# Values' products one step back in TensorE's order, in two attention stages of a three-block model kernel

## The chip, the cores and the metric

The kernel runs on one core of one Trainium2 chip. The metric is the device time of one launch in microseconds. A core has five engines that run their own instruction streams and wait for one another on semaphores: TensorE (PE in the profile, its weight loads PEld), VectorE (DVE), ScalarE (ACT), GpSimd (POOL) and SyncE (SP).

## The reference

The whole program is a first block (gated convolution and pooling mixer, cross attention to a memory, a mixture of 16 experts) and a second block of two layers. The change touches the attention of the two layers. Everything is float32, 256 tokens, width 1024.

```python
# layer 0: sparse attention, 16 heads of 64 in 4 groups; per head and token
o_cmp = softmax(q @ k_cmp) @ v_cmp          # 15 compressed blocks
o_sel = softmax(q_rot @ ks) @ vs            # causal; with 256 tokens all blocks are selected
o_win = softmax(q_rot @ kw) @ vw            # causal window, here all tokens
o = g0 * o_cmp + g1 * o_sel + g2 * o_win    # then o @ w_out
# layer 1: differential attention, 8 heads of 2 x 64, values of 128
a = softmax(q0 @ k0) - lam * softmax(q1 @ k1)
o = rms_norm(a @ v) * (1 - lam_init)        # then o @ w_out
```

## The kernel before

The kernel is written in engine streams: each engine has one hand-written order of instructions, and every dependence is a semaphore wait that is written out. Nothing is reordered by a planner. Activations lie transposed in SBUF, features in partitions, in one large tensor, `arena`. PSUM is split in two: `ring`, four banks that are filled in a fixed sequence of fills (`open_fill(f)` waits until the bank's previous fill is drained), and `acc[0]` to `acc[3]`, four banks that are used by hand.

Weights come in panels of 1 MB: SyncE loads them to `raw`, ScalarE and VectorE split them in a high and a low part (`w_hi`, `w_lo`, four slots each), and each dense product is three TensorE passes. Before an attention stage the four panels of the projection behind it are already split.

**Sparse attention.** 16 units: unit u is branch u % 2 (selected, then window) of the pair of heads u // 2. For each unit:
- TensorE: `n_scores(u)`, both heads, two banks of `ring` (12 matmuls); after the softmax `turn_three` for each of the two heads, six transposes of 128x128 in all, to `acc[2]` and `acc[3]`; then the values' products, 8 matmuls for an even unit and 12 for an odd one (the compressed branch is added there), to `acc[0]` or `acc[1]` by group of four heads.
- VectorE: `n_max(u)`, the row maxima from `ring` (L2143, L2144); `n_pt_odd(u)`, the copy of `acc[3]` to `arena` (L2192); `n_norm(u)`, reciprocal, gate and scaling of the probabilities (L2181 to L2186). Its order in iteration u is `n_max(u + 2)`, `n_pt_odd(u)`, the low part of a finished output (`out_lo`, L2196) where there is one, `n_norm(u + 1)`.
- ScalarE: the copy of `acc[2]` to `arena`, `out_hi` where a group is finished, and the exponentials `n_exp(u + 2)`.

The scores run two units ahead. TensorE's iteration u is: scores of u + 2, wait for the probabilities of u, transposes of u, wait for both copies of u, products of u.

**Differential attention.** 8 heads. The order is the same, with three transposes a head, to `acc[2]` for even heads (copied by ScalarE) and `acc[3]` for odd ones (copied by VectorE, L2333), six products of 128x128, and `busy_turn(h, n)`, n matmuls of the identity ahead of the transposes, whose result is overwritten; each shows as two instructions. VectorE's order is `d_max(h + 2)`, the copy for odd h, `d_norm(h + 1)` (L2314 to L2321). ScalarE's is, for even h, the copy and then `d_out` (copy and square of a finished pair of heads), and for every h `d_exp(h + 2)`.

All matmuls go through a helper `mm` and are recorded on L604, those of `turn_three` on L1008; all of ScalarE's activations are recorded on L1158.

Of the kernel before, what the change touches and what calls it, by code (L numbers as in the profile page):

```python
# [28 lines left out]
P = 128  # L29
T = 256  # L30
# [14 lines left out]
HEADS, HD, GROUPS = 16, 64, 4  # L45
DIFF_HEADS = 8
# [213 lines left out]
def program(nc, a, out):  # L260
# [5 lines left out]
    with ctx:  # L266
# [9 lines left out]
        def shared(name):  # L276

            tag, _, what = name.partition("_")
            if tag not in NORMS or what not in PER_NORM:
                return name, 0  # L280
            before = [t for t in NORMS[:NORMS.index(tag)] if not (t == "f" and what in ("scaled", "hi", "ready"))]
            return "norm_" + what, PER_NORM[what] * len(before)
# [5 lines left out]
        def S(name):  # L288

            name = shared(name)[0]  # L290
            if name not in sems:
                sems[name] = ctx.enter_context(nc.semaphore(name))
            return sems[name]
# [39 lines left out]
        def blk(i, n=1):  # L333
            return arena[:, i * T:(i + n) * T].rearrange("p (b t) -> p b t", b=n)

        def flat(i, off, n):
            return arena[:, i * T + off:i * T + off + n]

        ring = ctx.enter_context(nc.psum_tensor("ring", [P, BANKS * 512], F32))
        acc = [ctx.enter_context(nc.psum_tensor(f"acc{i}", [P, 512], F32)) for i in range(4)]  # L340

        def bank(f):
            return ring[:, (f % BANKS) * 512:(f % BANKS + 1) * 512]
# [54 lines left out]
        def n_p(u, o):  # L398

            return flat(N_P, (u % 2) * 768 + o * 384, 384)  # L400
# [14 lines left out]
        def d_pt(h):  # L415
            return flat(D_PT, (h % 2) * 384, 384)
# [182 lines left out]
        def _(pe):  # L599
# [3 lines left out]
            def mm(dst, lhs, rhs, start, stop, **kw):  # L603
                return nc.tensor.matmul(dst, lhs, rhs, start=start, stop=stop, **kw)  # L604
# [57 lines left out]
            def full(name, ready=None, norm=None):  # L662

                for i in range(FL_N[name]):
                    linear(PN[name] + i, FL[name] + i, KB, 2, lambda k: h_hi[:, k, :], lambda k: h_lo[:, k, :],
                           ready if i == 0 else None)
                    if norm and i:
                        stat_pair(norm, i - 1)
                if norm:
                    stat_pair(norm, FL_N[name] - 1)  # L670

            def stat_pair(tag, j, src=lambda k: blk(SQX, 8)[:, k]):

                f = FL[tag + "_stat"]
                if j == 0:
                    open_fill(f)
                pe.wait_ge(*sig(tag + "_squared", j + 1))
                for k in (2 * j, 2 * j + 1):
                    last = mm(bank(f)[:, 0:T], ones[:], src(k), k == 0, k == KB - 1)
                if j == KB // 2 - 1:  # L680
                    last.then_inc(S(tag + "_summed"), 1)
# [69 lines left out]
            for g in range(4):  # L751
                f = FL["pool_out"] + g
                open_fill(f)
                for b in range(2):
                    c = slice(g * 256 + b * P, g * 256 + (b + 1) * P)
                    o = bank(f)[:, b * T:(b + 1) * T]
# [23 lines left out]
            for h in range(X_HEADS):  # L780
# [11 lines left out]
                vals = blk(VALS, 8).rearrange("p (t c) n -> p t (c n)", t=2)  # L792
# [6 lines left out]
            def pairs_ready(sem):  # L799
                def ready(k):  # L800
                    if k % 2 == 0:
                        pe.wait_ge(*sig(sem, k // 2 + 1))
                return ready
# [196 lines left out]
            def n_scores(u):  # L1000
                b, br = divmod(u, 2)
                both_scores(n_s_fill(u), blk(N_QR, 8)[:, b, :], blk((N_KSD, N_KWD)[br], 4)[:, b // 2, :])\
                    .then_inc(S("n_scored"), 1)

            def turn_three(dst, src):

                for c in range(3):
                    last = nc.tensor.transpose(dst[:, c * P:(c + 1) * P], src[:, c * P:(c + 1) * P], ident[:])  # L1008
                return last
# [11 lines left out]
                last.then_inc(S("cmp_turned"), 1)  # L1021
            pe.wait_ge(S("cmp_pt_even"), 1)
            pe.wait_ge(S("cmp_pt_odd"), 1)
            for u in range(HEADS):
                b, br = divmod(u, 2)
                g = b // 2
                if u + 2 < HEADS:
                    n_scores(u + 2)
                pe.wait_ge(S("n_probs"), u + 1)
                for o, sem in ((0, "n_pt_even"), (1, "n_pt_odd")):  # L1030
                    if u > 0:
                        pe.wait_ge(S(sem), u)
                    turn_three(acc[2 + o], n_p(u, o)).then_inc(S("n_turned"), 1)
                if br == 0 and b % 2 == 0 and g >= 2:

                    pe.wait_ge(S("no_ready"), g - 1)
                pe.wait_ge(S("n_pt_even"), u + 1)
                pe.wait_ge(S("n_pt_odd"), u + 1)
                v = blk((N_VS, N_VW)[br], 2)
                dst = [acc[g % 2][o * HD:(o + 1) * HD, (b % 2) * T:(b % 2 + 1) * T] for o in range(2)]  # L1040
                for o in range(2):
                    mm(dst[o], v[:, 0, g * HD:(g + 1) * HD], n_pt(u, o)[:, 0:T], br == 0, False)
                for o in range(2):
                    mm(dst[o][:, P:T], v[:, 1, g * HD:(g + 1) * HD], n_pt(u, o)[:, T:T + P], False, False)
                if br == 1:
                    for o in range(2):
                        i = 2 * (b % 2) + o
                        last = mm(dst[o], blk(V_CMP)[32 * i:32 * i + NC, 0, g * HD:(g + 1) * HD],
                                  pt_cmp[32 * i:32 * i + NC, g, :], False, True)
                    last.then_inc(S("n_o_done"), 1)  # L1050
            full("n_o", pairs_ready("no_ready"), norm="m0")

            def mlp(l):
# [49 lines left out]
            def busy_turn(h, n):  # L1103

                for _ in range(n):
                    mm(acc[2 + h % 2][:, 0:T], ident[:], ident[:].unsqueeze(1).to_broadcast([P, 2, P]), True, True)
# [3 lines left out]
            d_scores(0)  # L1110
            d_scores(1)
            vals = blk(D_V, 8).rearrange("p (t c) n -> p t (c n)", t=2)
            for h in range(DIFF_HEADS):
                if h + 2 < DIFF_HEADS:
                    d_scores(h + 2)
                sem = ("d_pt_even", "d_pt_odd")[h % 2]
                if h >= 2:
                    pe.wait_ge(S(sem), h // 2)
                busy_turn(h, 6 if h == 0 else 2)
                pe.wait_ge(S("d_probs"), h + 1)  # L1120
                turn_three(acc[2 + h % 2], d_p(h, 0)).then_inc(S("d_turned"), 1)
                if h % 2 == 0 and h >= 4:

                    pe.wait_ge(S("s_squared"), h // 2 - 1)
                pe.wait_ge(S(sem), h // 2 + 1)
                dst = acc[(h // 2) % 2][:, (h % 2) * T:(h % 2 + 1) * T]
                v = vals[:, :, h * P:(h + 1) * P]
                mm(dst[:, 0:P], v[:, 0], d_pt(h)[:, 0:P], True, True)
                mm(dst[:, P:T], v[:, 0], d_pt(h)[:, P:T], True, False)
                mm(dst[:, P:T], v[:, 1], d_pt(h)[:, T:T + P], False, True).then_inc(S("d_o_done"), 1)  # L1130

            def sq_s_ready(b):
                pe.wait_ge(S("s_squared"), b // 2 + 1)
# [19 lines left out]
        def _(act):  # L1153
# [341 lines left out]
            for u in range(HEADS):  # L1495
                act.wait_ge(S("n_turned"), 2 * u + 1)
                func(n_pt(u, 0), acc[2][:, 0:3 * P], ACT.Copy).then_inc(S("n_pt_even"), 1)
                if u % 4 == 0 and u > 0:
                    out_hi(u // 4 - 1)
                if u + 2 < HEADS:  # L1500
                    n_exp(u + 2)
# [70 lines left out]
            def d_out(k):  # L1572

                act.wait_ge(S("d_o_done"), 2 * k + 2)
                o = acc[k % 2][:].rearrange("p (b t) -> p b t", b=2)
                func(blk(D_Q + 2 * k, 2), o, ACT.Copy).then_inc(S("d_o_out"), 1)
                func(blk(SQX + 2 * k, 2), o, ACT.Square).then_inc(S("s_squared"), 1)
# [3 lines left out]
            for h in range(DIFF_HEADS):  # L1581
                if h % 2 == 0:
                    act.wait_ge(S("d_turned"), h + 1)
                    func(d_pt(h), acc[2][:, 0:3 * P], ACT.Copy).then_inc(S("d_pt_even"), 1)
                    if h > 0:
                        d_out(h // 2 - 1)
                if h + 2 < DIFF_HEADS:
                    d_exp(h + 2)
            d_out(3)
# [8 lines left out]
        def _(dve):  # L1598
# [534 lines left out]
            for o in range(2):  # L2133
                h = slice(o * HD, (o + 1) * HD)
# [69 lines left out]
            for u in range(HEADS):  # L2204
                if u + 2 < HEADS:
                    n_max(u + 2)
                n_pt_odd(u)
                if u % 4 == 0 and u > 0:
                    out_lo(u // 4 - 1)
                if u + 1 < HEADS:  # L2210
                    n_norm(u + 1)
# [168 lines left out]
```

## Time and profile before

| | |
|---|---|
| median of 3 runs | 1569.76 us (1562.02 to 1571.52) |
| the profiled execution | 1571.11 us, of that 1569.4 us span from the first to the last instruction |
| mean granted TensorE clock | 0.954 of full |
| busy: PE, PEld, DVE, ACT, POOL | 1490.7, 1408.4, 955.6, 626.5, 76.0 us |
| sparse attention, first scores to last product | 856 to 929 us |
| differential attention, first scores to last product | 1287 to 1325 us |

A busy PE is not a PE at its peak: matmuls are pipelined and their ends are modelled. An engine's idle time costs something only where the chain of work that ended last runs through the engine that ends it.

### The profile page before, as it was taken

The numbers are of one execution on the slowest core, as the hardware profiler recorded it, in microseconds if no ns is written. First come the engines' busy times: TensorE is split into PE (matmuls) and PEld (weight loads), VectorE is DVE, ScalarE is ACT, GpSimd is POOL, SyncE is SP. The second block draws the span as 40 slices with busy tenths as digits, with TensorE's granted clock in tenths as the row PEclk, the third lists the DMA queues.
The fourth block names the chain that finished last, engine by engine and source line by source line (L and its number), as shares of the span: only waits on it lengthen the run. The fifth ranks groups of instructions, "written<-read, shape, count | busy, mean of one in ns | idle before, by whom it ended". The sixth has DMA issues, their size and how long they took to land.

```text
span 1569.4 us, 26439 instructions
## 1 busy us (share of the span) xinstructions
PE 1490.7 (95%) x11149; PEld 1408.4 (90%) x11149; DVE 955.6 (61%) x1175; ACT 626.5 (40%) x792; POOL 76.0 (5%) x113
## 2 busy tenths in 40 slices
PE   6999999999999999999998789999999998999998
PEld 5999999889999999998986568999989875899998
DVE  4569887644676777645416656788844475555543
ACT  3445454344344333434512544344334324344441
POOL 4013000001000000000000010000000000000000
PEclk9999999999999999979967899999979989999999
DMA  5565544443488788834510014999953520245651
GB/s 167 185 205 184 165 134 148 134 135 121 159 279 277 255 285 278 275 108 125 176 48 1 1 41 139 297 320 323 317 179 109 167 81 1 81 143 179 187 188 55
DMA packets 173574, 260.95 MB, mean 166 GB/s; under 512 B 5509, under 2 KB 148146, under 8 KB 173362
## 3 DMA queue, kind: packets, MB, share of 16 engines
q1 hardware_dynamic: 160480, 202.98, 40.1%
q0 software_dynamic: 10128, 51.30, 9.6%
q10 hardware_dynamic: 2882, 5.46, 1.2%
q8 instruction: 64, 1.05, 0.3%
q14 instruction: 20, 0.16, 0.0%
HBM read 258.67 MB, written 1.05 MB: 165 GB/s over the span
## 4 chain that ended last, share of the span: by engine, by line
PE 72%; DVE 12%; DMA 8%; ACT 5%; issue 2%; ACTq 1%; DVEq 0%; SPq 0%
PE ring L604 56%; PE acc L604 15%; DMA raw<-in_w_mlp_in_dram 6%; DVE w_lo L1610 4%; ACT w_hi L1158 3%; DVE arena L1656 1%; DVE arena L1747 1%; DMA vec_in<-in_nsa_pe_v_dram 1%; ACT arena L1158 1%; DVE norm L1625 1%; DVE h_lo L1650 1%; DVE arena L2192 1%; DMA raw<-in_diff_w_in_dram 1%; DVE arena L2113 0%; DVE arena L2110 0%
## 5 line engine op out<-in xcount | busy, mean ns | idle before, releaser
L1610 DVE TENSOR_TENSOR w_lo<-raw,w_hi 128x2048 fp32r<-128x2048 f32 (+1 forms) x191 | 437.0, 2289 | 353.6 <-ACT w_hi L1158 353.3
L604 PE MATMUL ring<-h_hi,w_hi 128*128 128x256 f32 x2088 | 599.5, 287 | 12.0 <-DVE h_lo L1650 7.5
L604 PE MATMUL ring<-h_lo,w_hi 128*128 128x256 f32 x2088 | 593.7, 284 | 0.0
L604 PE MATMUL ring<-h_hi,w_lo 128*128 128x256 f32 x2088 | 593.7, 284 | 0.0
L1158 ACT ACTIVATE w_hi<-raw 128x2048 fp32r<-128x2048 f32 (+1 forms) x191 | 363.3, 1902 | 252.2 <-DMA raw<-in_w_mlp_out_dram 62.2
L604 PEld LDWEIGHTS ring<-h_hi,w_hi 128*128 128x128 f32 x2088 | 404.0, 193 | 19.9 <-issue 8.0
L604 PEld LDWEIGHTS ring<-h_lo,w_hi 128*128 128x128 f32 x2088 | 403.9, 193 | 0.4
L604 PEld LDWEIGHTS ring<-h_hi,w_lo 128*128 128x128 f32 x2088 | 403.7, 193 | 0.0
L604 PE MATMUL acc<-e_hi,w_hi 128*128 128x256 f32 x768 | 219.0, 285 | 6.1 <-DVE e_lo L2236 3.8
L604 PE MATMUL acc<-e_hi,w_lo 128*128 128x256 f32 x768 | 218.7, 285 | 0.0
L604 PE MATMUL acc<-e_lo,w_hi 128*128 128x256 f32 x768 | 218.7, 285 | 0.0
L1158 ACT ACTIVATE arena<-ring 128x512 f32<-128x512 f32 (+3 forms) x118 | 69.0, 588 | 296.5 <-PE ring L604 291.5
L604 PEld LDWEIGHTS acc<-e_hi,w_hi 128*128 128x128 f32 x768 | 148.9, 194 | 6.5 <-DVE e_lo L2236 4.0
L604 PEld LDWEIGHTS acc<-e_lo,w_hi 128*128 128x128 f32 x768 | 148.9, 194 | 0.0
L604 PEld LDWEIGHTS acc<-e_hi,w_lo 128*128 128x128 f32 x768 | 148.9, 194 | 0.0
L1950 DVE SCALAR_TENSOR_TENSOR arena<-arena,cond 128x1536 f32<-128x1536 f32 x64 | 114.6, 1811 | 3.2 <-DMA arena<-in_w_ada_dram 3.1
L604 PE MATMUL ring<-k_ident 128*128 128x256 f32 x340 | 82.2, 399 | 2.5 <-DVE arena L1811 1.7
L604 PEld LDWEIGHTS ring<-k_ident 128*128 128x128 f32 x340 | 67.7, 201 | 14.3 <-DVE arena L1811 1.9
L566 POOL DMA_DIRECT2D arena<-in_w_ada_dram x64 | 33.9, 529 | 469.4 <-DVE arena L1950 467.8
L604 PE MATMUL acc<-arena 128*64 128x256 f32 (+4 forms) x240 | 34.4, 348 | 21.5 <-DVE arena L2192 15.1
L1747 DVE SCALAR_TENSOR_TENSOR arena<-arena,vec 128x256 f32<-128x256 f32 x120 | 54.7, 526 | 0.0
L1158 ACT ACTIVATE arena<-ring,stat 128x128 f32<-128x128 f32 (+1 forms) x104 | 42.8, 428 | 27.7 <-DVE stat L2144 18.6
(259 smaller groups left out, 1409.3 us busy)
## 6 DMA issues: line engine op xcount, KB each, us to landing
arena<-in_w_ada_dram POOLq DMA_DIRECT2D x64, 768.0 KB, 5.8
raw<-in_w_mlp_in_dram SPq DMA_DIRECT2D x32, 1024.0 KB, 5.7
raw<-in_w_mlp_out_dram SPq DMA_DIRECT2D x32, 1024.0 KB, 5.0
raw<-in_w_in_dram SPq DMA_DIRECT2D x24, 1024.0 KB, 5.2
raw<-in_w_e_gate_dram SPq DMA_DIRECT2D x16, 1024.0 KB, 5.5
raw<-in_w_e_up_dram SPq DMA_DIRECT2D x16, 1024.0 KB, 6.4
raw<-in_w_e_down_dram SPq DMA_DIRECT2D x16, 1024.0 KB, 6.1
raw<-in_diff_w_in_dram SPq DMA_DIRECT2D x12, 1024.0 KB, 5.1
```

The lines of the kernel that those rows point to most:

```text
L566: pool.dma_start(flat(ADA_RAW, (n % 2) * ADA_W, ADA_W), src).then_inc(S(f"ada_landed{n % 2}"), 16)
L604: return nc.tensor.matmul(dst, lhs, rhs, start=start, stop=stop, **kw)
L1158: return nc.scalar.activation(dst, src, fn, **kw)
L1610: tt(w_lo[q % SPL][:, 0:n], raw[q % RAW][:, 0:n], w_hi[q % SPL][:, 0:n].bitcast(F32), ALU.subtract)\
L1625: chain.did(nc.vector.reciprocal(norm[:, 2, :], norm[:, 1, :]))
L1650: last = stt(h_lo[:, b, :], blk(mid, 8)[:, b], shift(b), h_hi[:, b, :].bitcast(F32), ALU.add, ALU.subtract)
L1656: last = stt(blk(mid, 8)[:, b], x_t[:, b, :], gain(b), norm[:, row, :], ALU.mult, ALU.mult)
L1747: chain.did(stt(y[:, b], at, w, y[:, b], ALU.mult, ALU.add))
L1950: stt(dst, flat(ADA_RAW, (n % 2) * ADA_W, ADA_W), s, dst, ALU.mult, ALU.add).then_inc(S("ada_used"), 1)
L2192: nc.vector.tensor_copy(n_pt(u, 1), acc[3][:, 0:3 * P]).then_inc(S("n_pt_odd"), 1)
```

## The change

In both attention stages TensorE's order in iteration u becomes: scores of u + 2, wait for the probabilities of u, transposes of u, and then the products of u - 1, with their waits for the copies of u - 1. The products of the last unit stand behind the loop. Because the last product of a group is now issued one unit later, the output's high and low parts move one unit on in ScalarE's and VectorE's order. In the differential attention the filler matmuls become one a head (two before), and stand behind the products; the six at head 0 stay. No instruction that computes is added or left out.

```diff
+            def n_values(u):
                 b, br = divmod(u, 2)
                 g = b // 2
...
+            for u in range(HEADS):
+                if u + 2 < HEADS:
+                    n_scores(u + 2)
+                pe.wait_ge(S("n_probs"), u + 1)
+                for o, sem in ((0, "n_pt_even"), (1, "n_pt_odd")):
+                    if u > 0:
+                        pe.wait_ge(S(sem), u)
+                    turn_three(acc[2 + o], n_p(u, o)).then_inc(S("n_turned"), 1)
+                if u > 0:
+                    n_values(u - 1)
+            n_values(HEADS - 1)
...
             for h in range(DIFF_HEADS):
                 if h + 2 < DIFF_HEADS:
                     d_scores(h + 2)
                 sem = ("d_pt_even", "d_pt_odd")[h % 2]
                 if h >= 2:
                     pe.wait_ge(S(sem), h // 2)
-                busy_turn(h, 6 if h == 0 else 2)
+                if h == 0:
+                    busy_turn(h, 6)
                 pe.wait_ge(S("d_probs"), h + 1)
                 turn_three(acc[2 + h % 2], d_p(h, 0)).then_inc(S("d_turned"), 1)
...
+                if h > 0:
+                    d_values(h - 1)
+                    busy_turn(h + 1, 1)
+            d_values(DIFF_HEADS - 1)
...
-                if u % 4 == 0 and u > 0:
+                if u % 4 == 1 and u > 4:
                     out_hi(u // 4 - 1)
...
-                    if h > 0:
-                        d_out(h // 2 - 1)
+                elif h > 2:
+                    d_out(h // 2 - 1)
...
-                if u % 4 == 0 and u > 0:
+                if u % 4 == 1 and u > 4:
                     out_lo(u // 4 - 1)
```

`n_values` and `d_values` hold the statements that stood at the end of the loops' bodies, with their waits (`n_pt_even`, `n_pt_odd`, `no_ready`; `d_pt_even` or `d_pt_odd`, `s_squared`).

## Rows read from the trace of the kernel before

**Rows 1.** Part 4 of the page: shares of the chain by engine.

```profile
PE 72%; DVE 12%; DMA 8%; ACT 5%; issue 2%; ACTq 1%; DVEq 0%; SPq 0%
```

**Rows 2.** The chain in the sparse attention: start us, us on the chain, what.

```profile
866.00 1.29 PE acc L1008 x6
...
868.02 1.55 PE acc L604 x8
869.57 2.12 PE ring L604 x12
...
875.14 1.20 PE ring L604 x12
...
886.02 0.87 PE acc L604 x8
886.89 1.20 PE ring L604 x12
...
888.11 0.42 DVE stat L2143
...
889.05 0.56 DVE arena L2192
...
889.75 1.45 PE acc L604 x12
...
919.01 1.20 PE ring L604 x12
...
927.71 1.45 PE acc L604 x12
```

**Rows 3.** Timeline of the sparse attention: start, duration, instruction, [idle before, releaser].

```profile
883.09 0.52 PEld L604 LDWEIGHTS ring<-arena 64*128 64x128 f32 x8 [0.39 <-issue]
...
885.79 0.68 DVE L2196 TENSOR_TENSOR h_lo<-acc,h_hi 128x512 fp32r<-128x512 f32 x1
...
924.15 0.56 DVE L2192 COPY arena<-acc 128x384 f32<-128x384 f32 x1 [1.11 <-PE acc L1008]
924.63 0.17 DVE L2181 RECIPROCAL stat<-stat 128x4 f32<-128x4 f32 x1
...
925.69 0.35 DVE L2186 TENSOR_SCALAR arena<-arena,stat 128x256 f32<-128x256 f32 x1
...
926.09 0.88 PE L1008 MATMUL acc<-k_ident,arena 128*128 128x128 f32 x6 [0.36 <-DVE arena L2186]
```

**Rows 4.** Windows: stretch, length, busy PE, PEld, DVE, ACT, POOL, clock, DMA.

```profile
848.90:852.30 3.40, 3.40 (x11) 2.86 (x11) 1.53 (x4) 3.25 (x5) 0.00 (x0) 0.50 0.00 0
863.80:872.60 8.80, 8.05 (x44) 5.70 (x44) 3.70 (x11) 2.44 (x10) 0.00 (x0) 0.50 0.00 0
867.28:868.02 0.74, 0.00 (x1) 0.03 (x1) 0.66 (x3) 0.64 (x3) 0.00 (x0) 0.50 0.00 0
876.00:920.00 44.00, 32.92 (x310) 22.21 (x311) 31.93 (x102) 25.46 (x102) 0.00 (x0) 1.00 0.01 1
1298.00:1324.00 26.00, 21.36 (x153) 16.35 (x154) 16.40 (x50) 14.46 (x58) 0.00 (x0) 1.00 0.01 2
```

**Rows 5.** The chain in the differential attention, same columns as rows 2.

```profile
1297.21 0.34 PE acc L1008 x3
...
1299.05 1.19 PE ring L604 x12
...
1304.26 0.92 PE acc L604 x4
...
1305.54 0.50 ACT arena L1158
...
1315.04 1.19 PE ring L604 x12
...
1323.67 0.94 PE acc L604 x6
```

**Rows 6.** Timeline of the differential attention, VectorE's last instruction of a normalization.

```profile
1306.15 0.75 DVE L2321 SCALAR_TENSOR_TENSOR arena<-arena,stat 128x128 f32<-128x128 f32 x2
```

More of the change, by code:

```diff
@@ L1023, in _ @@
             pe.wait_ge(S("cmp_pt_odd"), 1)
-            for u in range(HEADS):
+            def n_values(u):
                 b, br = divmod(u, 2)
                 g = b // 2
[L1027 to L1033, printed above, removed]
                 if br == 0 and b % 2 == 0 and g >= 2:
@@ L1112, in _, with d_values @@
             vals = blk(D_V, 8).rearrange("p (t c) n -> p t (c n)", t=2)
+            def d_values(h):
+                if h % 2 == 0 and h >= 4:
+                    pe.wait_ge(S("s_squared"), h // 2 - 1)
+                pe.wait_ge(S(("d_pt_even", "d_pt_odd")[h % 2]), h // 2 + 1)
+                dst = acc[(h // 2) % 2][:, (h % 2) * T:(h % 2 + 1) * T]
+                v = vals[:, :, h * P:(h + 1) * P]
+                mm(dst[:, 0:P], v[:, 0], d_pt(h)[:, 0:P], True, True)
+                mm(dst[:, P:T], v[:, 0], d_pt(h)[:, P:T], True, False)
+                mm(dst[:, P:T], v[:, 1], d_pt(h)[:, T:T + P], False, True).then_inc(S("d_o_done"), 1)
             for h in range(DIFF_HEADS):
@@ L1118, in _ @@
                     pe.wait_ge(S(sem), h // 2)
-                busy_turn(h, 6 if h == 0 else 2)
+                if h == 0:
+                    busy_turn(h, 6)
                 pe.wait_ge(S("d_probs"), h + 1)
                 turn_three(acc[2 + h % 2], d_p(h, 0)).then_inc(S("d_turned"), 1)
[L1122 to L1130, printed above, removed]
+                if h > 0:
+                    d_values(h - 1)
+                    busy_turn(h + 1, 1)
+            d_values(DIFF_HEADS - 1)
             def sq_s_ready(b):
```

## The prediction

> **What bounds the kernel now.** I read the page's chain first: 72% of the span is TensorE's own work and only 12% VectorE's [rows 1]. A reordering can win only where TensorE waits, so I went on to the chain of the two stretches that the diff touches, 854 to 929 us (sparse attention, 16 units) and 1289 to 1325 us (differential attention, 8 heads). The reader is to see a relay in the first. TensorE ends the scores of unit u+2, VectorE takes their maxima (from 888.11) and then copies unit u's transposes (889.05 to 889.61), and only then do the values' products of unit u start, at 889.75 [rows 2]. From the end of the scores (886.89 + 1.20 = 888.09) to that start TensorE adds nothing to the chain; its transposes (six matmuls, some 0.9 us [rows 3]) run beside the maxima. An even unit costs 0.87 + 1.20 + 1.66 = 3.73 us, an odd one, with 12 products in place of 8, 1.45 + 1.20 + 1.66 = 4.31 us, a pair 8.04. In 876 to 920 us, 11 units, TensorE is busy 32.92 of 44 us, VectorE 31.93 [rows 4]. A head of the differential attention costs 0.94 + 1.19 + 0.92 + 0.34 + 0.02 + 0.50 + 0.04 = 3.95 us: products, scores, four filler matmuls, transposes, a gap, the copy by ScalarE, a gap [rows 5]; with VectorE's copy of 0.57 it takes 4.0.
>
> **The change in the sparse attention.** Nothing is added or removed; the products of unit u-1 move behind the transposes of unit u. The copy they need is then a whole unit old, so their wait for it goes. What is late next? The transposes of unit u+1 need its probabilities, and these stand on VectorE behind the maxima of u+2 and the copy of u. I work that out with e(n) for the end of the scores of unit n:
> - VectorE: maxima from e(u+2) + 0.02, the copy 0.94 later (888.11 to 889.05 [rows 2]), the normalization 0.47 after that (924.15 to 924.63), its length from 924.63 to 925.69 + 0.35 = 926.04, that is 1.41 us [rows 3]. So the probabilities of u+1 are done at e(u+2) + 2.84.
> - TensorE: the transposes that waited for such probabilities ended at 926.09 + 0.88 = 926.97, 0.93 us after them [rows 3]. Behind them now come the products of unit u and the scores of u+4.
> - For an odd u the loop is 2.84 + 0.93 + 1.45 + 1.20 = 6.42 us from e(u+2) to e(u+4), a pair. For an even u it is 0.87 in place of 1.45, 5.84. TensorE's own work for a pair, nothing waited for, is 2 x (1.20 + 0.64) + 0.87 + 1.45 = 6.00 us, where 0.64 is what the transposes add behind the scores (half of the 1.28 us that they added at half clock, 866.00 to 867.28 [rows 2]). VectorE's is at most 2 x 2.84 = 5.7. The longest is 6.42: TensorE stands some 0.4 us once in a pair, in place of 1.0 us (1.66 less 0.64) in every unit.
> - ScalarE has 25.46 us of work in those 11 units, 2.3 each [rows 4], less than the shortest unit. Its exponentials of u+2 follow the maxima of u+2 and are wanted by a normalization that stands a whole unit later, so I cost them at nothing; were that cover gone, they would lengthen the loop by what they are late. The two waits ahead of the products (both copies) are met long before: the copies end about a unit earlier.
> - The output's high and low parts move from u = 4, 8, 12 to u = 5, 9, 13, because the last product of their group is now issued one unit later. The low part takes 0.68 us on VectorE [rows 3], 0.60 of it net. Before, it lay in the time in which VectorE waited for scores; now it stands ahead of the normalization of an even unit, on the loop: + 0.60 each time. Queued behind it are that normalization and TensorE's transposes.
>
> From e(4) to e(15) before: 876.34 to 920.21, 43.9 us [rows 2]. After: five pairs, 32.1, two low parts, 1.2, and one unit of 3.7: 37.0 us. **Saved: 6.9.** The tail from e(15) to the last product was 920.21 to 929.16, 8.9 us. After: low part and normalization of 14 end at 3.44, transposes 4.37, copy and normalization of 15 at 6.29, transposes 7.22, products of 14 and 15, 0.87 + 1.45, 9.5 us. **Lost: 0.6.**
>
> **The start, at half clock.** From 863.8 to 872.6 the granted clock was 0.50 (1.2 GHz) [rows 4]. Unit 0 keeps its times up to 867.28. Then scores 3 follow at once: 867.28 + 2.12 = 869.40; transposes 1 (their probabilities are ready: maxima, copy and normalization take 2.84 us and began near 866.0, so an estimate of 869) + 1.28 = 870.68; products 0, + 1.55 = 872.23; scores 4 by 873.6 if the clock rises at 872.6 as now. That saves 2.7 us against 876.34. The clock can rise sooner, though. In 848.9 to 852.3, with TensorE busy throughout, it was 0.50 for 3.4 us, and full after that; in 863.8 to 872.6 there is a pause, 867.28 to 868.02, in which TensorE did nothing, and the half clock lasted 8.8 us [rows 4]. That pause is the very wait that the change takes out. With a rise near 869.3, e(4) is 869.4 + 0.64 + 0.87 + 1.20 = 872.1. **Saved: 4.2**, which I take; 2.7 is the other end. Sparse attention in all: 4.2 + 6.9 - 0.6 = 10.5 us (9.0 with the late rise).
>
> **The change in the differential attention.** Products one head back, and the filler is one matmul pair a head in place of two, set after the products. Four filler instructions took 0.92 us and were on the chain [rows 5], so a head is relieved of 0.46 us besides. TensorE's own work becomes 1.19 + 0.34 + 0.94 + 0.46 = 2.93 us a head.
> - VectorE: scores ended at 1304.26 [rows 5], the normalization behind them at 1306.15 + 0.75 = 1306.90 [rows 6], 2.64 us later, in an even head. In an odd one its copy stands between, 0.46 more by the sparse stage's 0.47: 3.10. Transposes behind a late normalization: half as many as in the sparse stage, so 0.93 less half of 0.64, 0.6 us.
> - Loop of a pair: 3.10 + 0.60 + 0.94 + 0.46 + 1.19 = 6.29 us, against 5.86 of TensorE's own and 8.0 now.
> - The first transposes end at 1297.55. Scores 3 ended at 1300.24 [rows 5], since products 0 waited for the copy and stood ahead; after, 1297.55 + 1.1 = 1298.7. **Saved: 1.5.**
> - Scores 3 to 7: 1300.24 to 1316.23 now, 16.0 us; after, two pairs, 12.6. **Saved: 3.4.**
> - Scores 7 to the last product: 8.4 us now; after, normalization of 6 at 3.10, transposes 3.70, products 5 and filler 5.10, transposes 7 at 5.55, products 6, filler, products 7: 7.9. **Saved: 0.5.**
> - ScalarE's output copy and square (about 1.1 us) move from even heads, where its transposes' copy stands too, to odd ones, where it has none. At half a unit of slack or more they cost nothing; without that cover the exponentials and the normalization of the next head slip by up to 1.1 us, three times. The filler after products 6 is now in the tail, 0.46, counted above.
>
> Together 5.4 us. Everything behind either stage is shifted whole: weights of the next panels are split already, and DMA moves almost nothing in both stages [rows 4]. **Sum: 10.5 + 5.4 = 15.9 us**, say 16. The profiled execution took 1571.1 us (span 1569.4): it would be 1555.1. The median of the runs shown is 1569.8, 1.3 below it, so the forecast is **1553.8**.
>
> **A rule that speaks against it.** TensorE was at the full clock through 876 to 920, though idle a quarter of the time in gaps of 1 us, and through 1298 to 1324 with the fillers, 21.36 of 26 us busy [rows 4]. The Trainium skill ("TensorE: Matmul & The Clock Gate", "A second HAM failure mode: psum-queue depth-cycling") says that frequent small idles between groups of matmuls can make the clock swing between its two levels. By that rule taking out fillers is a danger, and the time would be that of the first rival below; the trace disagrees at a share of 0.75. After the change I work out a busy TensorE in 6.0 of 6.4 us and in 5.9 of 6.3, over 0.9 in both stages.
>
> **The rivals.**
> - *The clock falls in one of the stages; slower than before.* A unit at half clock is TensorE's 2.12 + 1.28 + 1.55 = 4.95 us even or, by the same doubling, 6.3 odd, against 3.2 forecast: some 2.4 us lost in each. The gain is gone from the 7th of 22 such units, and over 12 make it over 1% slower, no more than 1590. For it: fewer fillers. Against it: the shares just given. 0.04.
> - *Late rise only*: everything else as worked out, 14.5 saved, 1555.3. 0.13.
> - *Small gaps*: TensorE's weight loads show 0.17 to 0.39 us put down to issue wherever its stream crosses a wait, and a unit gets no fewer waits in the new order. If 0.25 us of these, now hidden in the relay's wait, come bare in each of 22 units, 5.5 us are lost: 10.4 saved, 1559.4. 0.15.
> - *VectorE waits as well*: the output copies and the exponentials slip the normalization in every unit, and TensorE's wait for probabilities takes the old wait's place. With the loop of a pair at 7.2, half way to 8.04, the gain halves, 8 us: 1562. Against it: VectorE's chained work of a unit is at most 2.84 us in 3.2. 0.12, and with it the case that TensorE's stream already ran as if reordered and nothing moves (1570), which the copies that stand bare on the chain speak against [rows 2].
> - *TensorE's own bound*: the transposes start sooner than I price them, pairs are 6.0 and 5.9; 2.1 + 0.9 us more: 1550.8. 0.10.
> - My own sum: 0.44. The rest, 0.02, is a run-to-run shift.
>
> **How the numbers follow.** The single executions of before spread from 1562.0 to 1571.5, and about 1% (15.7 us) is what a measurement of this kernel can tell from no change. My sum lies on that bound, so somewhat over half of the 0.44 counts as faster (0.27), TensorE's own bound whole (0.10), of the late rise two fifths (0.05) and of the small gaps a little (0.01): 0.43. Slower by over 1% is three quarters of the first rival, 0.03; within 1% is the rest, 0.54. The range goes from below TensorE's own bound, 1550.8 less some 4 us of spread, to the halved gain, 1562, plus 2: 1547 to 1564. Outside it are the slow clock, the case in which nothing moves, and the ends of the spread, under 0.2.
>
> **What would show it.** Right: the chain in 876 to 920 is nearly all TensorE, the idle of products on the copy is gone, transposes wait some 0.4 us on the normalization once a pair, e(15) - e(4) near 37 us, the half clock ends near 869, last product ended near 918.6, and the differential stage ends 5.4 us nearer to its beginning. Wrong: transposes that wait in every unit; a granted clock below 1.00 inside either stage; ScalarE late for the normalization.

## The result, and the profile after

The changed kernel took 1553.3 us (median of 10 runs) against 1568.7 us for the kernel before (10 runs). The ratio of the two sets of runs is 0.9908, 95% interval 0.9880 to 0.9935, that is 14.4 us less (10 to 19); the medians lie 15.3 us apart. The forecast was 1553.8. The profiled execution took 1556.4 us, 14.7 less than the 1571.1 of before.

The lines of the changed kernel are renumbered: maxima are L2156 and L2157, the copy by VectorE L2205, the normalization L2194 to L2199, the low part L2209, in the differential attention L2327 to L2334 and L2346. The chain in the sparse attention (start us, us on the chain, what), two pairs of units, the second with a low part:

```profile
873.61 1.20 PE ring L604 x12
...
874.84 0.42 DVE stat L2156
...
875.78 0.55 DVE arena L2205
876.32 0.10 DVE stat L2194
...
877.39 0.27 DVE arena L2199
877.66 0.04 issue
877.70 0.88 PE acc L1008 x6
878.58 1.38 PE acc L604 x12
879.96 1.20 PE ring L604 x12
...
882.58 0.68 DVE h_lo L2209
...
884.32 0.27 DVE arena L2199
884.60 0.04 issue
884.64 0.87 PE acc L1008 x6
885.51 1.38 PE acc L604 x12
886.89 1.20 PE ring L604 x12
```

The chain before went through every unit and left TensorE for the maxima and the copy each time [rows 2]. Now it leaves TensorE once in a pair, and comes back through the normalization (877.66) to the transposes, as the forecast's loop has it: scores end 874.81, scores two units on end 881.16, a pair of 6.35 us where 8.04 stood; the pair with the low part is 881.16 to 888.09, 6.93. Even units' products and scores are no longer on it at all. In 876 to 906 us TensorE waits for the normalization at the transposes of every second unit, 0.26 us, or 0.85 where the low part stands ahead of it. The windows of the changed kernel, columns as in [rows 4]:

```profile
861.78:868.60 6.82, 5.74 (x32) 4.00 (x33) 3.96 (x15) 3.24 (x13) 0.00 (x0) 0.52 0.00 0
876.00:906.00 30.00, 27.52 (x258) 17.60 (x256) 26.43 (x86) 20.81 (x87) 0.00 (x0) 1.00 0.01 1
1281.40:1288.20 6.80, 6.06 (x22) 4.63 (x23) 4.13 (x14) 2.21 (x12) 0.00 (x0) 0.50 0.42 134
1290.00:1304.00 14.00, 12.75 (x109) 9.35 (x107) 12.24 (x37) 11.34 (x48) 0.00 (x0) 1.00 0.01 2
```

TensorE is busy 27.5 of 30 us where it was 32.9 of 44 [rows 4]. VectorE, 26.4 of 30, is the next that has little left. The third row is new: half clock at the start of the differential attention for 6.8 us, against 3.4 before.

**Where the time went.** I measure a stage from its first row maxima to its last product, in the profiled execution of each kernel:

| us | before | after | difference |
|---|---|---|---|
| up to the sparse attention | 857.4 | 856.5 | -0.9 |
| sparse attention | 71.75 | 60.64 | -11.1 |
| between the two | 359.6 | 362.1 | +2.5 |
| differential attention | 35.9 | 30.5 | -5.4 |
| behind it, to the end of the span | 244.8 | 245.0 | +0.2 |

The two stages gained 16.5 us, where the forecast had 15.9. The 2.5 us between them stand in code that the change doesn't touch; they are taken up below, as is how much of the 16.5 us is the clock's.

### The profile page after: what moved, and what is told of

Read it like the earlier page. It is cut to its first block, busy times and chain, and to the rows that moved or that the text cites. A ratio compares the mean times of both kernels' runs of the same rounds, so it can differ in the third digit from the quotient of the medians.

```text
span 1554.7 us, 26417 instructions
## 1 busy us (share of the span) xinstructions
PE 1485.9 (96%) x11135; PEld 1403.0 (90%) x11135; DVE 955.1 (61%) x1175; ACT 626.1 (40%) x792; POOL 76.0 (5%) x113
## 3 DMA queue, kind: packets, MB, share of 16 engines
q1 hardware_dynamic: 160480, 202.98, 40.2%
## 4 chain that ended last, share of the span: by engine, by line
PE 71%; DVE 13%; DMA 8%; ACT 5%; issue 2%; ACTq 1%; DVEq 0%; SPq 0%
PE ring L604 56%; PE acc L604 14%; DMA raw<-in_w_mlp_in_dram 6%; DVE w_lo L1623 4%; ACT w_hi L1171 3%; DVE arena L1669 1%; DMA vec_in<-in_nsa_pe_v_dram 1%; DVE arena L1760 1%; PE acc L1008 1%; DVE norm L1638 1%; DVE h_lo L1663 1%; ACT arena L1171 1%; DMA raw<-in_diff_w_in_dram 1%; DVE arena L2126 0%; DVE arena L2123 0%
## 5 line engine op out<-in xcount | busy, mean ns | idle before, releaser
L1171 ACT ACTIVATE e_hi<-arena 128x512 fp32r<-128x512 f32 x48 | 29.9, 622 | 59.1 <-DVE arena L1980 59.1
L604 PE MATMUL ring<-arena 64*128 64x128 f32 (+4 forms) x322 | 47.4, 362 | 5.4 <-ACT arena L1171 5.4
```

What stands on the lines that cost most here:

```text
L1171: return nc.scalar.activation(dst, src, fn, **kw)
```

## The experiments

e1, e2, e8 and e10 were executed six or twelve times each, the others once. Single executions of one kernel differ by 10 us and more, so the single ones are read by their stages, not by their times, which were 1550.6 (e3), 1560.0 (e4), 1547.4 (e5), 1544.4 (e6), 1558.0, 1544.5 and 1557.6 (e7, e7b, e7c) and 1560.0 us (e9). The table has one execution of each, the profiled one. For the sparse attention it cuts the stage at e(5) and e(15), the ends of the scores of units 5 and 15, and says when TensorE's clock fell (us behind the end of the first scores) and for how long it stayed at 0.50; the last columns are the same for the differential attention.

| kernel | order, sparse | to e(5) | to e(15) | tail | stage | fell, for | differential | fell, for |
|---|---|---|---|---|---|---|---|---|
| before | old | 22.6 | 40.2 | 9.0 | 71.8 | 5.2, 10.2 | 35.9 | 4.7, 3.4 |
| changed | new | 18.3 | 32.9 | 9.4 | 60.6 | 5.1, 6.8 | 30.5 | 3.0, 6.8 |
| e1 | new | 18.2 | 32.9 | 10.2 | 61.3 | 3.2, 6.8 | 35.7 | 3.4, 3.4 |
| e2 | old | 20.7 | 40.2 | 9.0 | 69.8 | 3.2, 6.8 | 29.2 | 3.7, 3.4 |
| e3 | new | 18.0 | 32.9 | 9.4 | 60.3 | 6.1, 3.4 | 28.2 | 4.0, 3.4 |
| e4 | new | 18.2 | 32.9 | 9.4 | 60.5 | 3.2, 6.8 | 30.8 | 4.6, 3.4 |
| e5 | low part later | 18.0 | 31.7 | 8.8 | 58.5 | 6.0, 3.4 | 29.2 | 4.5, 3.4 |
| e6 | copies by ScalarE | 17.9 | 29.4 | 8.0 | 55.3 | 5.2, 6.8 | 29.0 | 3.4, 3.4 |
| e7 | first relay kept | 19.0 | 32.9 | 9.4 | 61.3 | 3.2, 6.8 | 29.3 | 4.7, 3.4 |
| e7b | the same | 19.0 | 32.9 | 9.4 | 61.3 | 2.8, 6.8 | 30.5 | 3.0, 6.8 |
| e7c | the same | 18.9 | 32.9 | 9.4 | 61.2 | 6.1, 3.4 | 30.6 | 3.2, 6.8 |
| e8 | as e6 | 17.1 | 29.4 | 8.0 | 54.5 | 3.2, 6.8 | 28.2 | 3.8, 3.4 |
| e9 | old | 20.6 | 40.1 | 9.0 | 69.7 | 6.1, 3.4 | 33.4 | 3.4, 3.4 |
| e10 | as e6 | 17.1 | 29.4 | 8.0 | 54.5 | 6.1, 3.4 | 29.9 | 3.3, 6.8 |

**e1 and e2: each half of the change alone.** e1 is the changed kernel with the differential attention's two loops (TensorE's and ScalarE's) as before; e2 is the kernel before with these two loops as changed.

> The new order in the sparse attention alone; the differential attention as before. Stage lengths from the first row maxima to the last product. Theory (each stage gains by itself): sparse 60.6 us as in the changed kernel (71.7 before), differential 35.8 as before, total 11 us below before, ratio 0.993. Rival (part of the gain is the state in which the program reaches the second stage, its clock or its weights): the differential stage moves too, by 1 us or more.

> The new order and the single filler in the differential attention alone; the sparse attention as before. Theory: sparse 71.7 us, differential 30.4 as in the changed kernel, total 5 us below before, ratio 0.9965. Rival: the differential stage gains less than 5 us when the first stage is not shortened.

e1: 1558.9 us, ratio 0.9947 (0.9919 to 0.9974); e2: 1560.3 us, ratio 0.9966 (0.9941 to 0.9991), both against 1564.5 us for the kernel before on their chip. Each half gains in its own stage and leaves the other's steady part alone (e1's differential attention 35.7, e2's middle of the sparse attention 40.2), so the theory stands. e2's sparse stage is 69.8 us, not the 71.7 expected, and its differential one 29.2, not 30.4: in both the half clock at the start was shorter than in the execution that the expectation was read from. e1's total fell short of the 11 us expected, with the interval reaching to 12.7; its stage did not. One number of e1 was not expected: a tail of 10.2 in place of 9.4. Two windows of e1 (busy PE, clock):

```profile
914.70:918.10 3.40, 1.43 (x14) 0.99 0.00 0
918.10:921.90 3.80, 3.73 (x19) 0.56 0.00 0
```

TensorE waited two microseconds for the normalization of unit 14, the clock fell behind that, and transposes and products of the tail ran at 1.2 GHz for 3.4 us. In the six other executions with the same tail (the changed kernel, e3, e4 and the three of e7) it was 9.4 us, and the clock did not fall there.

**e3 and e4: the fillers in the new order.** Each changes one line behind the products.

```diff
-                    busy_turn(h + 1, 1)
```

in e3, and in e4

```diff
-                    busy_turn(h + 1, 1)
+                    busy_turn(h + 1, 2)
```

> The changed kernel without the one filler a head in the differential attention (the six at head 0 stay). Theory: TensorE is busy enough without it; the clock stays at 1.00 from the third scores on; the filler adds about 0.2 us to the loop of a pair, so the pair goes from 6.06 to 5.86 us and the stage from 30.4 to about 29.5. Rival (frequent small idles make the clock swing): the granted clock falls to 0.50 inside the stage and the stage is over 32 us.

> The changed kernel with two fillers a head behind the products in place of one. Theory: the loop of a pair passes through one of its two fillers, the other lies in TensorE's wait for the normalization: pair 6.06 to about 6.3 us, stage 30.4 to about 31.2. Rival A (every filler is on the path): pair 6.5 or more, stage 32 or more. Rival B (the fillers fill waits only): pair and stage unchanged.

The chain of e3, of the changed kernel and of e4, from transposes that waited to the end of the next scores:

```profile
1289.01 0.52 PE acc L1008 x3
1289.53 0.67 PE acc L604 x6
1290.20 1.20 PE ring L604 x12
```

```profile
1293.73 0.52 PE acc L1008 x3
1294.25 1.10 PE acc L604 x8
1295.35 1.20 PE ring L604 x12
```

```profile
1295.89 0.52 PE acc L1008 x3
1296.41 1.53 PE acc L604 x10
1297.94 1.20 PE ring L604 x12
```

Six products take 0.67 us in the dense stream, with two instructions of one filler 1.10, with four 1.53: 0.43 us for a filler, not the 0.2 I had expected; so e3's stage came out at 28.2 us, not 29.5, and its pair at 5.63, not 5.86. The pair is 5.63, 6.06 and 6.49 us, 0.43 apart, although each pair holds two heads: one of its two fillers is on the loop and the other lies in TensorE's wait for the normalization. So the theory's mechanism holds, and rival A's pair of 6.5 was met for another reason, the size. Against the stages with the same 3.4 us of half clock (29.2 in e2 and e5), e3 saved 1.0 us and e4 cost 1.6. Without fillers TensorE was busy 12.99 of 15 us and the clock stayed full, as it did behind the start of this stage in e8 and e10, which have none either:

```profile
1283.00:1298.00 15.00, 12.99 (x113) 9.88 (x112) 12.16 (x38) 11.30 (x47) 0.00 (x0) 1.00 0.01 2
```

The swing between the two levels that the Trainium skill describes ("TensorE: Matmul & The Clock Gate", "A second HAM failure mode: psum-queue depth-cycling"), and that the prediction weighed as the danger of fewer fillers, did not come in this run.

**e9: one filler in the old order.** `busy_turn(h, 6 if h == 0 else 1)` in the kernel before.

> The kernel before, with one filler a head in place of two in the differential attention, nothing else. Theory (in the old order the fillers are bare on the chain, 0.92 us for two): a head costs 0.4 to 0.46 us less and the stage is 33.0 us in place of 35.8, so about half of the 5.4 us of that stage is the fillers' and half the order's. Rival (the filler hides in another wait): 35.8.

The stage went from 35.9 (35.7 in e1) to 33.4 us. So of the 6.6 us by which the new loops shorten the stage at like clock (35.8 to 29.2), 2.4 come with the filler taken out first and 4.2 with the order. Taken the other way round, by e4, which has the new order and still two fillers, the order brings 5.0 us (35.8 to 30.8) and the filler 1.6, since one of a pair's two fillers then lies in a wait. The change bundles two things; a quarter to a third of its second half is not the order's.

**e5: the low part behind the normalization.**

```diff
+                if u + 1 < HEADS:
+                    n_norm(u + 1)
                 if u % 4 == 1 and u > 4:
                     out_lo(u // 4 - 1)
-                if u + 1 < HEADS:
-                    n_norm(u + 1)
```

> The changed kernel with the output's low part behind the next unit's normalization in VectorE's order, not ahead of it. Theory (the low part stands on the loop of its pair): the two pairs that took 6.93 us take 6.35, the third low part leaves the tail, and the sparse stage goes from 60.6 to about 58.9 us. Rival (it only moves to the next maxima): the pairs keep 6.9 us and the stage 60.6.

All pairs now take 6.34 us. The chain of a pair that had 6.93 before:

```profile
885.20 0.42 DVE stat L2156
...
886.13 0.55 DVE arena L2205
...
888.06 0.87 PE acc L1008 x6
888.93 1.38 PE acc L604 x12
890.31 1.20 PE ring L604 x12
```

The low part is not on it. Against e3, whose clock fell at the same moment, the stage is 1.9 us shorter, as expected (1.7).

**e6: VectorE's copy given to ScalarE.** On top of e5:

```diff
                 func(n_pt(u, 0), acc[2][:, 0:3 * P], ACT.Copy).then_inc(S("n_pt_even"), 1)
+                act.wait_ge(S("n_turned"), 2 * u + 2)
+                func(n_pt(u, 1), acc[3][:, 0:3 * P], ACT.Copy).then_inc(S("n_pt_odd"), 1)
...
-                n_pt_odd(u)
```

> As the kernel with the low part behind the normalization, and besides the odd head's copy in the sparse attention is done by ScalarE, behind its even head's copy, so that VectorE's chain is maxima and normalization alone. Theory: that chain is 0.47 us shorter, the loop falls below TensorE's own work, a pair takes 5.9 to 6.0 us in place of 6.35, TensorE waits for nothing in the middle of the stage, and the stage is about 57 us. Rival (ScalarE becomes late: 2.8 us of work in a unit of 3.0): the exponentials hold up the normalization and a pair takes 6.3 us or more.

```profile
881.73 0.66 PE acc L1008 x6
882.39 0.80 PE acc L604 x8
883.19 1.19 PE ring L604 x12
884.37 0.67 PE acc L1008 x6
885.04 1.38 PE acc L604 x12
886.42 1.19 PE ring L604 x12
```

The chain is now TensorE alone, and its windows show it busy all the time:

```profile
874.00:904.00 30.00, 30.00 (x288) 19.52 (x286) 24.41 (x85) 26.19 (x107) 0.00 (x0) 1.00 0.01 2
```

A pair takes 5.88 us, just the sum of the lines above. This settles what held the changed kernel: VectorE's chain of maxima, copy and normalization. Take 0.47 us a unit out of it and TensorE's own work is the bound, with ScalarE at 26.2 of 30 us still not late. The stage, 55.3 us, came out 1.7 below the expectation, because the tail shortens as well (9.4 to 8.0).

**e7, e7b, e7c: the first relay kept.** The changed kernel, with `n_values(0)` inside iteration 0, ahead of scores 3, and the later ones as changed.

> The changed kernel, but the products of unit 0 stand ahead of the scores of unit 3 as before, with their wait for the copies; all other units in the new order. Theory (the pause behind the first transposes is what kept TensorE at 1.2 GHz): the granted clock is 0.50 for about 9 to 10 us from the drop, as before (10.1), in place of 6.9, and the stage is 2 to 3 us longer than 60.6. Rival (the earlier rise was a chance of its timing): the clock is back after about 6.9 us and the stage is 1 us longer at most, for the 0.74 us of the pause.

> The same kernel as in the run with the products of unit 0 ahead of scores 3, looked at once more, since the clock's fall came at another moment (3.2 us after the first scores' end, 5.2 in the kernel before). If it comes near 5.2 us: with the pause as the cause the half clock lasts about 10.2 us and the stage is near 64 us; without it 6.8 us and 61. If it comes at another moment, the run doesn't tell.

> The same kernel once more, with the same expectation as the look before it.

The clock came back after 6.8, 6.8 and 3.4 us, and it had fallen 3.2, 2.8 and 6.1 us behind the first scores. The other kernels whose clock fell at about 3.2 (e1, e2, e4, e8) or at 6.1 (e3, e5, e9, e10) had the same 6.8 and 3.4, old order or new. So the pause alone does not keep the clock low; the moment of the fall goes with the length. Only for a fall near 5.2 us do old and new order differ, 10.2 us before against 6.8 in the changed kernel and in e6, and in none of the three executions did the clock fall there. So whether the pause prolongs the half clock for a fall at that moment was not tested and stays open. What the first relay alone costs, at the same fall, is 0.85 us to e(5) (19.0 against 18.2, 18.9 against 18.0).

**e8 and e10: all that helped, together.** e8 is e6 and e3; e10 has ScalarE copy the odd heads of the differential attention too.

```diff
-                if h % 2 == 0:
-                    act.wait_ge(S("d_turned"), h + 1)
-                    func(d_pt(h), acc[2][:, 0:3 * P], ACT.Copy).then_inc(S("d_pt_even"), 1)
-                elif h > 2:
+                act.wait_ge(S("d_turned"), h + 1)
+                func(d_pt(h), acc[2 + h % 2][:, 0:3 * P], ACT.Copy).then_inc(S(("d_pt_even", "d_pt_odd")[h % 2]), 1)
+                if h % 2 and h > 2:
                     d_out(h // 2 - 1)
```

> The new order with the low part behind the normalization, ScalarE's copies of both heads in the sparse attention, and no filler a head in the differential attention. If the edits add up: sparse stage 55.3 us (53.0 where the half clock at its start is the short one), differential 28.1, together 23 to 25 us below the stages of before, ratio near 0.985. Rival (the time saved in the attention is given back in the weight loads of the stages behind): ratio above 0.990.

> As the combined kernel, and in the differential attention ScalarE copies the odd heads' transposes too. Theory: VectorE's chain of an odd head is 0.47 us shorter, the pair goes from 5.62 to about 5.15 us and the stage from 28.1 to about 27. Rival (ScalarE's 3.3 us of work in the heads with an output copy and square hold it up): the pair stays at 5.6 us.

e8: 1547.0 us, ratio 0.9871 (0.9830 to 0.9912). e10: 1545.1 us, ratio 0.9863 (0.9828 to 0.9898), against 1566.3 us before. Both are faster than before beyond their intervals; they overlap the changed kernel's interval, 0.9880 to 0.9935, in part, so only the stages say that they beat it: 82.6 us for both stages in e8, 91.1 in the changed kernel, 107.6 before. The stages of e8 gain 25.0 us as expected, its time 20.2 (13.8 to 26.6): the rival, that the rest gives some of it back, is neither shown nor excluded. In e10 the pair went to 5.2 us as expected, but the stage, 29.9 us, missed the 27 expected. Of this some 1.3 us are its longer half clock at the start; for the rest, e(3) to the last product is 18.5 us against 18.2 in e8. Its chain says why:

```profile
1289.60 0.53 PE acc L1008 x3
1290.13 0.02 issue
1290.15 0.03 ACT arena L1170
1290.18 0.36 issue
1290.54 2.28 ACT arena L1170 x9
```

ScalarE's copy and exponentials are now the chain, and in the tail behind e(7), 8.1 us against 7.0, they give back what the pairs won.

## Why the prediction was right

The mechanism was right, and the sum was right by terms that cancel. The measured gain holds 1.8 us of sparse attention that came from the longest half clock of the three old-order executions (71.8 us before, where e2 and e9 took 69.8 and 69.7), and lacks 1.2 us of differential attention that went to a long one after. At like clock the stages gain 9.3 us (69.8 to 60.5 in e2 and e4, 69.7 to 60.3 in e9 and e3) and 6.6 us (35.8 to 29.2), where the forecast had 10.5 and 5.4. That the median came within half a microsecond of the forecast is luck: the measured interval is 8.6 us wide.

- *The relay and what is late next.* Right. The copy left the chain, the normalization took its place once in a pair, and even units run free. Pair 6.35 against 6.42, with the low part 6.93 against 7.02; the 0.07 is the products' 1.45 us, which take 1.38 behind transposes. One sign I named for it was wrong: the chain in that stretch is not nearly all TensorE's. It has 53% of the chain in 876 to 906 us, VectorE nearly all the rest, and so it must be in a loop in which VectorE has 2.84 of 6.42 us.
- *e(4) to e(15).* 36.5 us (871.19 to 907.70) against 37.0; saved 7.4, not 6.9.
- *Tail.* 9.4 against 9.5.
- *Start.* 4.2 us forecast; e(4) came 5.1 us earlier on the span's clock, 4.2 after the 0.9 by which the stage began earlier. The size is right for this pair of executions, and the half clock ended at 868.4 us. The reason I gave, that the pause keeps the clock low, is not shown: e2 and e9 kept the pause and were back after 6.8 and 3.4 us. I had also misread the row: the half clock of before lasted 10.2 us, from 862.55, and not 8.8; it fell in TensorE's wait ahead of scores 2, before the pause. With a fall at 3.2 or 6.1 us the start saves 2.5 us (20.7 to 18.2, 20.6 to 18.0), the size of my rival of the late rise. With a fall near 5.2 it saved 4.3 (22.6 to 18.3), and whether the 1.8 us between are the pause's or chance is the part that e7 left open.
- *Low part on the loop.* Right: 0.58 us in each of its pairs, forecast 0.60, taken away by e5.
- *Differential attention.* 5.4 forecast and 5.4 measured, by two errors that cancel. The products' term was mis-sized: I took 0.94 us from a row in which TensorE had waited ahead of them [rows 5]; in a dense stream they take 0.67. The transposes behind the wait came out 0.06 us longer and the filler 0.03 shorter than priced. So the pair was 6.06, not 6.29, and the stage at like clock 29.2. The profiled execution lost 1.3 us of that to 6.8 us of half clock at the stage's start. By parts, the forecast saved 1.5, 3.4 and 0.5 us up to e(3), to e(7) and behind it; measured are 0.3, 3.9 and 1.3.
- *ScalarE's cover.* It held in the sparse attention, even with its work grown by half a microsecond a unit in e6, and broke in the differential attention when e10 did the same.
- *The clock rival.* Behind the start of both stages the clock stayed at 1.00, in the differential attention without fillers too. It fell once in a tail (e1), which cost 0.8 us, far from the 16 that this rival needed.
- *Small gaps.* None of 0.25 us a unit: a unit of e6 is its busy parts and nothing else.

## The two microseconds between the stages

The stretch between the two attentions runs the same instructions in every kernel here, and took 353.7 us (e2) to 365.7 us (e7c). TensorE's longest wait in it, in e2, the changed kernel and e7c (who waited for whom: total us, times, longest):

```profile
PE acc L604 <- DVE e_lo L2244: 0.9, 1, 0.9
```

```profile
PE acc L604 <- DVE e_lo L2249: 6.3, 3, 5.0
```

```profile
PE acc L604 <- DVE e_lo L2251: 10.0, 1, 10.0
```

Before it was 3.8 us. What holds VectorE's `e_lo` is the split of a panel of the next projection's weights, which stands ahead of it in its order, and that waits for the panel. On the chain of e2 and of e7c the load of this panel shows as:

```profile
1131.89 6.65 DMA raw<-in_diff_w_in_dram
```

```profile
1120.20 13.81 DMA raw<-in_diff_w_in_dram
```

It is the last of fourteen loads of 1 MB that stand on the chain one behind the other, each started when the split of a panel before it was done. In thirteen of the fourteen executions (e3's chain runs elsewhere) the first of them begins 53.1 us behind the last product of the sparse attention. Their times add up to 100.3 us in e2, 103.2 before, 106.2 in the changed kernel and 109.4 in e7c, and TensorE's wait grows with them, 0.9, 3.8, 5.0 and 10.0 us. The clock adds to it: at half clock the stretch spent 23.9 us in e2, 30.7 in the changed kernel and the one before, 37.5 in e7c. So the 2.5 us are a longer wait for weights.

Is that a part of the gain given back? The chain of loads hangs on the end of the attention by the same 53.1 us in old and new order, so an earlier end moves it whole; this speaks for scatter in the loads. The lengths alone can't tell: the old order stood in front of 353.7, 357.0 and 359.6 us (e2, e9, before), the new one in front of 355.8 to 365.7 (eleven executions). The ranges overlap, and the new order's mean, 361.2, is some 4.5 above the old one's, 356.8. Why the loads took longer in some executions is not shown.

The stretch ahead of the sparse attention, which no run here changed, scatters as much. The first row maxima came at 850.3 us (e7b) to 863.6 us (e1), and the half clock ahead of them added up to 71.7 and 99.0 us. Half of these 27.3 us, 13.6, is about the whole difference. The two stretches are much of why single executions differ by 10 us and more.

## What to carry to other kernels

When a hand-written order makes TensorE wait for a copy of its own result, put one unit of other work between the two, and then follow the chain once around: the next wait is on whatever engine stands behind that copy, and its length says how much of the gain stays. Price a TensorE step that moves into a dense stream by a row in which it ran densely, not by one that begins after a wait (six products: 0.67 us against 0.94). And where a change bundles an order with fewer fillers, run each alone, or the order is credited with both.

## What was not expected of the hardware

- The half clock at a stage's start lasted 3.4, 6.8 or 10.2 us in runs of nearly the same instructions, going with the moment of its fall behind the first scores (2.8 to 6.1 us); in the sparse attention a fall at 2.8 to 3.2 gave 6.8, one at 6.0 to 6.1 gave 3.4, in every execution; in the differential attention one at 3.0 to 3.3 gave 6.8 and one at 3.4 to 4.7 gave 3.4. This alone moves a stage by up to 2 us, and a comparison of two single traces has to take it out first.
- A wait of 2.0 us was followed by a fall of the clock in e1, and not in six other executions with the same code there.
